# Weight places in an attention stage: a two-layer model on one Trainium2 core, where two further places of the weight ring are opened earlier, twelve modulation pieces run inside the attention, and expert weights are requested before the routing

## The reference, cut to what matters

```python
for layer in range(DEPTH):                       # DEPTH = 2
    m_lat = _modulation(cond_lat, w_mod[layer], b_mod[layer])   # cond @ w + b, w is 1024 x 6144
    u_lat = _modulate(h_lat, m_lat[0], m_lat[1])
    if is_even:   # layer 0: attention over 768 keys and a pooling branch, then @ w_mix_out
        y_lat, y_ctx = _attn_pool_mixer(...)
    else:         # layer 1: short convolution between @ w_conv_in and @ w_conv_out
        y_lat = _short_conv_mixer(...)
    h_lat = _post_norm(h_lat, m_lat[2] * y_lat, ...)
    f_lat = _expert_choice_ffn(_modulate(h_lat, m_lat[3], m_lat[4]), w_router[layer], ...)
    h_lat = _post_norm(h_lat, m_lat[5] * f_lat, ...)

def _expert_choice_ffn(u, w_router, w_g, w_u, w_d):
    cap = CAPACITY_FACTOR * n // N_EXPERTS       # 64 tokens for each of 16 experts
    aff = jax.nn.softmax(einsum('bnd,de->ben', u, w_router), axis=1)
    gate, idx = lax.top_k(aff, cap)              # each expert picks its tokens
    xe = u[bidx, idx]
    ye = (silu(xe @ w_g) * (xe @ w_u)) @ w_d * gate   # three 1024 x 1024 matrices an expert
```

## Time and profile before

| | |
|---|---|
| median of three runs | 3001.9 us (2999.2 to 3005.44) |
| the profiled execution | 2999.43 us, span 2997.6 us |
| mean granted TensorE clock | 0.967 of full speed |
| PE busy | 2741.8 us, 91% of the span |
| VectorE, ScalarE, GpSimd busy | 1172.1, 806.2, 127.4 us |
| DMA | 601.06 MB, mean 201 GB/s |
| chain that ended last | PE 71%, DMA 13%, DVE 11%, ACT 4%, issue 1% |
| issues of expert weights | 192 pieces of 2048 KB, median 13.9 to 16.5 us to landing |

### The profile page before, as it was taken

How to read it: one execution, slowest core, us unless ns; L and a number is a source line. 1 busy time by engine, 2 the same in 40 slices (tenths; PEclk the granted TensorE clock), 3 DMA queues, 4 the chain that set the end, 5 groups by cost and what they waited for, 6 DMA issues and landing times.

```text
span 2997.6 us, 32112 instructions
## 1 busy us (share of the span) xinstructions
PE 2741.8 (91%) x13436; PEld 1789.1 (60%) x13436; DVE 1172.1 (39%) x1704; ACT 806.2 (27%) x1240; POOL 127.4 (4%) x124
## 2 busy tenths in 40 slices
PE   6887899988889979999888998999999999999998
PEld 4534544433368544443336777878778756787886
DVE  4454521211164451111126654333333588633333
ACT  2343311100031131110014433222232465522222
POOL 1210200000000110000001010000010000000000
PEclk9998899999999979999998999999999899999999
DMA  8860499999943069999991212222232300132320
GB/s 299 319 218 16 192 395 428 427 428 423 425 156 110 19 263 396 428 428 428 428 414 67 85 45 96 84 96 87 85 125 52 85 1 1 57 108 72 108 91 36
DMA packets 125648, 601.06 MB, mean 201 GB/s; under 512 B 7440, under 2 KB 12880, under 8 KB 100672
## 3 DMA queue, kind: packets, MB, share of 16 engines
q1 hardware_dynamic: 120128, 584.27, 49.3%
q0 software_dynamic: 5376, 14.75, 1.6%
HBM read 596.90 MB, written 2.10 MB: 200 GB/s over the span
## 4 chain that ended last, share of the span: by engine, by line
PE 71%; DMA 13%; DVE 11%; ACT 4%; issue 1%; POOL 0%; DVEq 0%; SPq 0%; ACTq 0%; POOLq 0%
PE psum L295 68%; DMA weight_ring<-in_w_exp_down 5%; DVE scratch L245 4%; ACT scratch L283 4%; PE psum L310 3%; DMA scratch<-in_w_exp_down 3%; DMA weight_ring<-in_w_exp_up 2%; DMA scratch<-in_w_exp_up 2%; DVE scratch L3627 1%; DVE scratch L278 1%; DVE scratch L258 1%; DMA weight_ring<-in_w_mix_in 1%; DVE scratch L1399 1%; DVE h L245 1%; DVE scratch L1810 0%
## 5 line engine op out<-in xcount | busy, mean ns | idle before, releaser
L295 PE MATMUL psum<-scratch,scratch 128*128 128x512 f32 (+13 forms) x9096 | 1885.0, 407 | 78.7 <-DVE scratch L245 22.0
L295 PEld LDWEIGHTS psum<-scratch,scratch 128*128 128x128 f32 (+4 forms) x9096 | 1369.3, 183 | 558.0 <-issue 235.5
L295 PE MATMUL psum<-weight_ring,scratch 128*64 128x512 f32 (+2 forms) x2752 | 646.0, 609 | 76.3 <-DMA weight_ring<-in_w_exp_down 26.6
L295 PEld LDWEIGHTS psum<-weight_ring,scratch 128*64 128x64 f32 (+2 forms) x2752 | 210.7, 140 | 467.0 <-issue 368.7
L283 ACT ACTIVATE scratch<-psum 128x512 f32<-128x512 f32 (+4 forms) x330 | 192.9, 585 | 1016.5 <-PE psum L310 557.7
L245 DVE TENSOR_TENSOR scratch<-weight_ring,scratch 128x2048 fp32r<-128x2048 f32 (+2 forms) x110 | 241.9, 2199 | 493.1 <-ACT scratch L283 491.8
L283 ACT ACTIVATE scratch<-weight_ring 128x2048 fp32r<-128x2048 f32 (+2 forms) x122 | 218.7, 1793 | 579.9 <-PE psum L295 556.7
L245 DVE TENSOR_TENSOR scratch<-scratch,psum 128x512 f32<-128x512 f32 x92 | 63.3, 688 | 532.2 <-PE psum L295 530.8
L310 PE MATMUL psum<-consts,scratch 128*128 128x128 f32 x1116 | 175.8, 300 | 64.8 <-DVE scratch L245 46.8
L245 DVE TENSOR_TENSOR scratch<-scratch,scratch 128x512 fp32r<-128x512 f32 (+12 forms) x355 | 199.5, 562 | 60.5 <-ACT scratch L283 43.0
L310 PEld LDWEIGHTS psum<-consts,scratch 128*128 128x128 f32 x1116 | 137.6, 166 | 132.3 <-DVE scratch L245 52.6
(11 more groups left out here) (106 smaller groups left out, 727.7 us busy)
## 6 DMA issues: line engine op xcount, KB each, us to landing
weight_ring<-in_w_exp_gate SPq DMA_DIRECT2D x44, 2048.0 KB, 15.8
weight_ring<-in_w_exp_down SPq DMA_DIRECT2D x44, 2048.0 KB, 14.2
weight_ring<-in_w_exp_up SPq DMA_DIRECT2D x43, 2048.0 KB, 15.6
weight_ring<-in_ffn_w SPq DMA_DIRECT2D x28, 2048.0 KB, 7.8
weight_ring<-in_w_mod SPq DMA_DIRECT2D x24, 2048.0 KB, 10.6
scratch<-in_w_exp_up SPq DMA_DIRECT2D x21, 2048.0 KB, 16.5
scratch<-in_w_exp_gate SPq DMA_DIRECT2D x20, 2048.0 KB, 15.8
scratch<-in_w_exp_down SPq DMA_DIRECT2D x20, 2048.0 KB, 13.9
```

The costliest lines, as they stand in the source:

```text
L295: ins = T.eng.matmul(out, lhsT, rhs, start=start, stop=stop)
```

## The change

Three things are changed. `RoutedModulation` is gone: the plain `Modulation` runs as the attention's filler, so that all 12 pieces of layer 1 are multiplied in steps 0 to 11. `Attention.sync` opens the two `more` places ahead of piece 2 and puts them at the front of the list. `Experts.sync` no longer opens the `more` places in layer 0 (they are open already); in layer 1 it opens them at the end of the convolution instead of at the end of mixout1. In both layers it now requests as many pieces as the list has places, five, before it waits for the end of mixout and opens the lent places.

```diff
-    def widen(self, Y, stage):
+    def widen(self, Y, stage, at):
         for name in ("pe", "dve", "act"):
             Y.wait_ge(*self.k.at("end", stage, name))
-        self.slots += [len(self.base) + i for i in range(len(self.more))]
+        self.slots[at:at] = [len(self.base) + i for i in range(len(self.more))]
...
-class RoutedModulation(Modulation):
...
 class MixerOut(Nothing):
...
-        if self.rest:
-            self.rest.rest_sync(Y)
...
-        if self.rest:
-            self.rest.first_pe(T)
         self.next.turn_pe(T, NT - 1)
...
 class Attention(Nothing):
     def sync(self, Y):
         for j in range(self.filler.steps):
+            if j == 2:
+                self.k.ring.widen(Y, AttnInputs.KEY, 0)
             self.filler.step_sync(Y, j)
...
 class Experts(Nothing):
     def sync(self, Y):
-        if not self.rest:
-            k.ring.widen(Y, self.before)
-        k.ring.lend(Y, self.before)
+        if self.layer:
+            k.ring.widen(Y, ShortConv.KEY, 1)
+        free = len(k.ring.slots)
         for what, e in self.order():
...
                 for i in range(2):
+                    if free == 0:
+                        k.ring.lend(Y, self.before)
+                    free -= 1
                     k.ring.load(Y, (self.key, name, e, i), long_rows(d[name][self.layer, e], i))
...
-        if self.rest:
-            self.rest.rest_pe(T)
...
-        if self.rest:
-            self.rest.rest_act(A)
...
-        if self.rest:
-            self.rest.rest_dve(V)
...
-    rest = RoutedModulation(k, 1, mods[1], Attention.TURNED)
-    attention = Attention(k, m0, inputs, rest)
+    attention = Attention(k, m0, inputs, Modulation(k, 1, mods[1], Attention.TURNED))
```

More of the change, by code:

```diff
@@ L880, with __init__ @@
 class MixerOut(Nothing):
-    def __init__(self, k, key, before, m, w, xT, gain, bias, layer, heads=False, rest=None):
+    def __init__(self, k, key, before, m, w, xT, gain, bias, layer, heads=False):
         self.k, self.key, self.before, self.w, self.xT, self.heads = k, key, before, w, xT, heads
@@ L887, in __init__ @@
         self.next = None
-        self.rest = rest
     def sync(self, Y):
@@ L1566, with __init__ @@
     ROUTING = (0, 3)
-    def __init__(self, k, layer, m, before, rest=None):
-        self.k, self.layer, self.before, self.rest = k, layer, before, rest
+    def __init__(self, k, layer, m, before):
+        self.k, self.layer, self.before = k, layer, before
         self.key = ("experts", layer)
@@ L3718, in plan @@
     inputs = AttnInputs(k, m0, first, base)
-    rest = RoutedModulation(k, 1, mods[1], Attention.TURNED)
-    attention = Attention(k, m0, inputs, rest)
+    attention = Attention(k, m0, inputs, Modulation(k, 1, mods[1], Attention.TURNED))
     stages = [Start(k, mods), inputs, attention]
     k.arena.at = top
-    stages.append(MixerOut(k, "mixout0", Attention.KEY, m0, d["w_mix_out"], m0["catT"], "ln_mix_g", "ln_mix_b", 0, heads=True,
-                           rest=rest))
+    stages.append(MixerOut(k, "mixout0", Attention.KEY, m0, d["w_mix_out"], m0["catT"], "ln_mix_g", "ln_mix_b", 0, heads=True))
     for layer, m in enumerate(mods):
@@ L3731, in plan @@
             k.arena.at = base
-        experts = Experts(k, layer, m, f"mixout{layer}", None if layer else rest)
+        experts = Experts(k, layer, m, f"mixout{layer}")
         stages[-1].next = experts
```

## The result

| | before | after |
|---|---|---|
| median beside each other on one chip | 3003.02 us | 3014.55 us |
| lowest and highest of seven executions | 2999.2 and 3005.44 us, and one of 14146.01 | 3006.28 and 3021.31 us |
| ratio, 95% interval | | 1.0038 (1.0026 to 1.005) |
| profiled execution, its span | 2999.43, 2997.6 us | 3006.28, 3004.5 us |

The change makes the kernel slower by 0.38%, 11.4 us (7.8 to 15.0). The forecast was 3017, from a sum of 15.0 us, with a range of 3009 to 3024. One execution of before took 14146.01 us, for a reason that no trace shows; without it before's median would be 3002.5.

A forecast was written before the change was run, and what follows sets the result against it. The prediction took the expert stages as bound by the weight transfers at about 428 GB/s and the attention by its own engine loop. Terms 6.4 + 7.7 + 0.9 = 15.0 us on 2999.43 gave 3014.4, as a median 3017, range 3009 to 3024.

The forecast's parts named there:

- The experts: Expert stages, both layers: sixth piece waits for the first one's place, so the last landing comes 3.2 us later each, +6.4.
- The slow restart: Rival, expert stages: the queue refills at 395 GB/s, 6.9 us a layer, 22.4 in all, or 3024; chance 0.09.
- the head start kept: Rival, expert stages: three early pieces come straight off the 96, 29.4 us gained, -20.8 in all, or 2981; chance 0.04.
- the lag that is eaten: Rival, expert stages: lag 0 in both layers, attention blocks at full clock, 5.2 us in all, or 3007; chance 0.06.
- The attention: Attention steps 9 to 12: three added product blocks make these steps take 40.68 us instead of 33.02, a cost of 7.7.
- The first rival: Attention: added products run inside PE's idle time and cost nothing, attention -3.4, +3.9 us in all, or 3005.8; chance 0.09.
- the two low-clock blocks: Attention steps 9 and 11: at full clock these product blocks would cost 3.3 us less, 4.3 in all, the lower end.
- The two places opened ahead of piece 2: Attention's requests: SyncE waits for the end of the input stage before this request; put at nothing, 2 us either way.
- Mixout and routing: Layer 0, mixout0 and routing: taking out three modulation pieces costs 0.9 us, as layer 1's stretch shows; bounds -1.9 and +0.9.

The follow-up runs named there:

- e2: Kernel after, but expert pieces requested as in before, all after the end of mixout into seven free places; median 3005.13 us, ratio 1.0015 to before.
- e3: Kernel after, but the two lent places put at the front of the list instead of its end; median 3008.21 us, ratio 1.0023 to before.
- e1: Kernel after once more with no edit, timed beside before on another occasion; median 3017.72 us, ratio 1.0052 to before.
- e4: Kernel after, with ScalarE's copies of the pooling product and of the values both moved earlier; median 2992.13 us, ratio 0.9971 to before.
- e5: Kernel after, with only ScalarE's copy of the pooling product moved to the end of its own step; median 3001.26 us, ratio 1.0018 to before.
- e6: Kernel before, with both ScalarE copies (pooling product and values) moved earlier; median 2988.07 us, ratio 0.9961 to before.

## Why the prediction was right, and where it was not

**The experts: 6.4 predicted, 6.5 measured.** 458.53 - 455.08 = 3.45 in layer 0 and 457.51 - 454.44 = 3.07 in layer 1, for 3.2 in each. The mechanism is as described: the sixth piece gets the first one's place, 3.75 us behind the first product (3.7 predicted), and the queue is full from 394 to 440 us at 427 GB/s. e2 and e3 show both halves of it, that the lag goes with the order of the places and that the head start has no value of its own. The slow restart (395 GB/s), the head start kept and the lag that is eaten (0 in both layers) are out.

The number came closer than the reasoning deserved, in two ways. First, two errors of about 1 us cancelled. At the landing of the fifteenth piece the lag is 4.4 us in layer 0 and 4.1 in layer 1, not 3.2: in layer 0 the restart costs 8.5 us from issue to landing, not 7.4 (7.5 in layer 1, where the nine transfers behind it take 45.3 instead of 44.1). Then before does not run "without a break": from the fifteenth to the 25th landing it takes 50.26 and 50.09 us, where after takes 49.16 and 48.95, and so 1.1 us come back. Second, the 44.6 us of the fifteenth piece in before, from which the 3.2 are worked out, hold a half clock of PE in both layers that isn't there in every run. Against 41.4, as in e2's layer 0 and in both layers of e3, the lag is 6.5 us (layer 0, e1 against e2) and 5.1 (layer 1, e1 against e3). Before and after alone were not enough to see this.

**The attention: 7.7 predicted, 7.2 measured in this profile,** and 9.7, 8.4 and 9.5 in e1, e2 and e3, which share its attention. In steps 9 to 12 alone, for which the 7.7 was worked out, it is 7.45, 7.1, 8.7 and 7.0; the rest is the clock in steps 6 to 8. Steps 9 and 11 took 10.34 and 10.30, step 10 took 14.36, for 10.47, 10.47 and 14.27, and step 12 took the 5.47 expected. Reading the new steps off steps 6 and 7 of the old trace held to 0.2 us here, and that closely by luck: in e1 steps 9 and 11 took 8.8 and 11.5 us, in e2 10.4 and 11.5, by how much of the step ran at the low clock. The reason given for the wait, the bank that waits for ScalarE's queued copy, is shown by e4 and e5 and not only argued.

The first rival, that the products would fill idle time, was wrong for this kernel, and what it rests on is right. Its condition was that the bank be free before the idle time. e4 and e6 fulfil it, and the three blocks cost nothing within 0.1 us. The prediction had the two low-clock blocks as the only part of the 7.7 that could go; in truth the blocks were hideable altogether, and so were twelve further microseconds that the kernel before already lost (64.11 against 51.53). The two places opened ahead of piece 2, put at nothing with 2 us either way, cost nothing: VectorE waits 6.00 us for the bias where it waited 5.98, and the maximum of step 6 comes at 170.51, before at 170.65.

**Mixout and routing: 0.9 predicted, 0.0 measured.** This step failed. From the last tile's first transposes to the first expert product it took 379.49 - 338.60 = 40.89 before, and 386.45 - 345.56 = 40.89 after; from the last logits, as the prediction counts, 42.59 in both, where it had 43.46 for after. The idle time of 1.84 us came to the digit, but the transposes behind it took 1.23 us, not layer 1's 1.98 at a granted clock of 0.50, and the whole stretch copied layer 0. "Layer 1 is the after-kernel's layer 0 in all that matters" was false for the clock: that a stretch ran at half clock in one layer is no property of the instructions. That the block was off the path, which the sign rests on, was right.

**The sum.** 6.5 + 7.2 + 0.0 = 13.7; the last landing of layer 1 is 13.4 us later. The span is only 6.9 us longer, since from there to the end before took 1436.89 us and after 1430.33, in code that the change doesn't touch. In e1 the same stretch takes 1440.41, in e3 1438.28, and the mean granted clock of e1 is 0.960 beside 0.967. The medians lie at +11.5 and, in e1, at +16.3, on both sides of 15.0: two measurements of the same kernel, 4.8 us apart, which is three quarters of the experts' term. So the sum was right in size, and a comparison of the two spans alone would have halved it.

## What to carry to other kernels

Loading ahead of a stage paid nothing here, because the queue of transfers ran empty behind it: find the piece whose place comes free last, and look whether the queue is empty there; a head start ends there. When a new place joins a rotating list, put it at the front, or it is filled only after the places ahead of it have been used. Where PE waits for a bank, ask what the copy that frees it is queued behind; here moving two copies a few rows up in ScalarE's program was worth some 13 us in the kernel before (e6), more than any piece of weights that was moved, and it made the moved work free. And look at several traces of a stage before a difference of 3 us in it is put down to a change: the clock alone moved the fifteenth piece by 3.2.

## What the runs showed that had not been expected

**Large transfers hold up small ones.** In mixout1 the three early pieces are requested from 1007.45 to 1008.31 us, and GpSimd requests the small loads of this stage from 1007.93 to 1011.10. The router's weights (1008.97) then take 18.5 us from issue to landing, and VectorE waits; in before they take 4.3, and in e2, which differs from after only in when and into which places the expert pieces are requested, 4.5. VectorE's row after, and the same one before:

```profile
1029.30 0.57 DVE L245 TENSOR_TENSOR scratch<-scratch,scratch 128x8 f32<-128x8 f32 x3 [14.60 <-DMA scratch<-in_ln_mix_b]
```

```profile
1004.78 0.57 DVE L245 TENSOR_TENSOR scratch<-scratch,scratch 128x8 f32<-128x8 f32 x3 [0.74 <-DMA scratch<-in_ln_mix_b]
```

It costs nothing here: from layer 0's last landing to layer 1's first product it takes 271.67 us, 271.75 before. What it costs where VectorE is the bound no run here shows.

**The rate.** Reads from HBM ran at 419 to 429 GB/s, mostly at 427 to 428, over the whole slices of 75 us inside the expert stages of every kernel, which runs on one core. The Trainium skill ("DMA: Bandwidth & Descriptors", section "Where 436 GB/s comes from") has the HBM side bind at about 358, a limit per core; the same section has a measurement of 425 for 16 MB, and the runs here agree with that. With 358 the lag would have been 11.8 us a layer by the prediction's estimate, where 3.45 and 3.07 were measured.

**The clock.** The same idle time of 3.26 us ahead of the same block was followed by a block of 1.92 us at 2.4 GHz, or by one of 3.07 to 3.64 us that ran for the most part at 1.2, from step to step and run to run. What a step behind an idle time costs can't be read off one trace.
